# Two chained blocks in float32 on one core: row transposes and weight splits placed elsewhere around the attentions

## Time and profile before

| | |
|---|---|
| profiled execution, its own time | 2446.54 us |
| its span in the trace | 2444.8 us |
| median of the three runs | 2446.37 us |
| TensorE busy (matmuls) | 2380.5 us, 97% |
| VectorE busy | 1629.9 us, 67% |
| ScalarE busy | 1128.9 us, 46% |
| GpSimd busy | 167.0 us, 7% |
| share of TensorE in the chain that ended last | 88% |
| mean granted TensorE clock | 0.999 of full |

### The profile page before, as it was taken

One profiled execution on the slowest core, in us unless ns is written; L12 is line 12 of the kernel. 1 busy time (PEld: TensorE's weight loads), 2 busy tenths in 40 slices (PEclk: granted clock), 3 DMA queues, 4 the chain that ended last, 5 costly groups with the idle time before them and its releaser, 6 DMA issues.

```text
span 2444.8 us, 33463 instructions
## 1 busy us (share of the span) xinstructions
PE 2380.5 (97%) x13600; PEld 2002.2 (82%) x13600; DVE 1629.9 (67%) x2282; ACT 1128.9 (46%) x1571; POOL 167.0 (7%) x182
## 2 busy tenths in 40 slices
PE   7999999999999999999999999999999989999999
PEld 5788887787888778887888878888888878888887
DVE  6766755547667576677776676777676666677664
ACT  3644344444443434436434355564443454574442
POOL 2100002021000320000100100000100000001000
PEclk9999999999999999999999999999999999999999
DMA  6365343343553445543654344344754434444652
GB/s 233 134 215 206 138 172 138 138 173 134 194 206 138 173 166 196 207 158 123 244 203 161 128 172 170 140 174 146 275 206 156 151 115 162 173 173 168 235 172 89
DMA packets 258776, 419.08 MB, mean 171 GB/s; under 512 B 11937, under 2 KB 149153, under 8 KB 258625
## 3 DMA queue, kind: packets, MB, share of 16 engines
q1 hardware_dynamic: 253760, 400.15, 46.4%
q0 software_dynamic: 4864, 16.80, 1.9%
HBM read 415.86 MB, written 1.05 MB: 171 GB/s over the span
## 4 chain that ended last, share of the span: by engine, by line
PE 88%; DVE 6%; ACT 3%; issue 2%; DMA 1%; POOL 1%; SPq 0%; DVEq 0%; ACTq 0%
PE bank_L L2343 19%; PE bank_L L2359 17%; PE bank_S L2688 7%; PE bank_T L2653 7%; PE bank_L L2653 7%; PE bank_O L2688 7%; PE bank_T L2658 4%; PE bank_L L2658 4%; PE bank_L L2340 4%; DVE wlo L1565 2%; PE bank_O L2343 1%; PE bank_O L2605 1%; PE bank_S L2343 1%; ACT whi L1188 1%; PE bank_T L2300 1%
## 5 line engine op out<-in xcount | busy, mean ns | idle before, releaser
L1565 DVE TENSOR_TENSOR wlo<-raw,whi 128x2048 fp32r<-128x2048 f32 x316 | 713.7, 2279 | 149.2 <-ACT whi L1188 148.8
L1188 ACT ACTIVATE whi<-raw 128x2048 fp32r<-128x2048 f32 (+1 forms) x294 | 549.3, 1894 | 51.4 <-DMA raw<-in_w_in 12.9
L2343 PE MATMUL bank_L<-whi,xt 128*128 128x512 f32 (+1 forms) x1600 | 494.0, 391 | 4.5 <-DVE wlo L1565 2.5
L2359 PE MATMUL bank_L<-whi,xt 128*128 128x512 f32 x1280 | 400.2, 394 | 6.9 <-DVE wlo L1565 5.2
L2343 PEld LDWEIGHTS bank_L<-whi,xt 128*128 128x128 f32 x1600 | 293.5, 189 | 64.0 <-issue 4.5
L2343 PE MATMUL bank_L<-wlo,xt 128*128 128x512 f32 (+1 forms) x800 | 309.0, 386 | 0.0
L2359 PEld LDWEIGHTS bank_L<-whi,xt 128*128 128x128 f32 x1280 | 237.9, 189 | 56.7 <-issue 7.3
L2359 PE MATMUL bank_L<-wlo,xt 128*128 128x512 f32 x640 | 250.5, 391 | 0.0
L1440 ACT ACTIVATE tok<-tok 128x256 f32<-128x256 f32 x96 | 40.1, 417 | 450.6 <-DVE tok L2059 450.6
L2653 PE MATMUL bank_T<-xt,whi 128*128 128x512 f32 x768 | 192.3, 392 | 0.0
L2653 PE MATMUL bank_L<-xt,whi 128*128 128x512 f32 x768 | 191.7, 392 | 0.0
(11 more groups left out here) (344 smaller groups left out, 3654.4 us busy)
## 6 DMA issues: line engine op xcount, KB each, us to landing
raw<-in_w_gate_up SPq DMA_DIRECT2D x176, 512.0 KB, 5.7
raw<-in_w_in SPq DMA_DIRECT2D x72, 1024.0 KB, 7.0
draw<-in_w_down SPq DMA_DIRECT2D x44, 1024.0 KB, 5.8
raw<-in_ffn_w_up SPq DMA_DIRECT2D x88, 512.0 KB, 5.6
raw<-in_b_w_qkv SPq DMA_DIRECT2D x36, 1024.0 KB, 7.0
draw<-in_ffn_w_down SPq DMA_DIRECT2D x22, 1024.0 KB, 5.9
raw<-in_w_lift SPq DMA_DIRECT2D x16, 1024.0 KB, 6.2
raw<-in_a_w_qkv SPq DMA_DIRECT2D x12, 1024.0 KB, 8.8
```

The source lines that it names most:

```text
L1188: act.activation(wide(whi, w, nkc, ncols)[:, ks, :], wide(raw, w, nkc, ncols)[:, ks, :], ACT.Copy) \
L1565: dve.tensor_tensor(wide(wlo, w, nkc, ncols)[:, ks, :], wide(raw, w, nkc, ncols)[:, ks, :], wide(whi, w, nkc, ncols)[:, ks, :].bitcast(F32 ...
L2343: mm = pe.matmul(banks[name][:, 0:st["ncols"]], xx[:, kk, t * P:(t + 1) * P], ww[:, kk, :], start=(kk == 0 and q == 0), stop=(kk == nkc - ...
L2359: mm = pe.matmul(banks[bank][:, :], xx[:, k, t * P:(t + 1) * P], ww[:, k, :], start=(k == 0 and q == 0), stop=(k == KC - 1 and q == 2))
```

## The change

- **Second block, turns.** A new kind of stage, `turn_within`: the turns of `kd`, of the memory query and of the selected attention's query are issued by TensorE inside the product that stood ahead of them, at t = 1 and two k-steps from its end, and copied by ScalarE ahead of that product's second evacuation.
- **Memory attention.** `split_lo` of the lift chunk's halves goes from steps 1 and 4 to steps 4 and 5, the fourth `best` from step 5 to step 6. ScalarE's `split_hi` stays in steps 1 and 4.
- **Recurrence.** In the second layer VectorE makes the low part of the chunk of gate 0 half 1 inside `decay_logs`, ahead of its last four instructions instead of behind them.
- **Layers 0 and 3.** The rows leave by groups of four heads: TensorE turns group 0 after the values of unit 14, group 1 ahead of the values of unit 15, group 2 behind them, group 3 in the middle of the first output product. ScalarE copies groups 0 and 1 ahead of the output of unit 15. VectorE makes the low parts of groups 0, 1, 2, then the first half of chunk w+1, then group 3.
- GpSimd makes the high part of chunk w+1 (four casts per layer) in place of ScalarE.

```diff
@@ attention with sinks, where the stages are listed
-                o_is = attention(units, [(turn_done, n["turn"]), (dev, n["dev"])], first, behind, in_twos=True)
+                hv = halves(r)
+                pool_splits([n["w"] + 1])
+                attention(units, [(turn_done, n["turn"]), (dev, n["dev"])], first, behind, in_twos=True, turned=hv)
...
-            lhs = (tlo_done, [[hv["at"]["sg"] + k // 2 + 1 for k in range(KC)]] * T, (xt_hi, xt_lo)) if att else \
-                split(r, o_is, (xt_hi, xt_lo))
+            lhs = (tlo_done, [[hv["at"]["sg"] + k // 2 + 1 for k in range(KC)]] * T, (xt_hi, xt_lo))
...
-            lhs = renorm("layer", r, ALPHA, lhs, wo, bias, begun=att)
+            lhs = renorm("layer", r, ALPHA, lhs, wo, bias, begun=att, groups=hv)
@@ in attention(): when each group may be turned
+            if turned:
+                for g in range(4):
+                    turned["at_tp"][g] = n["tp"]
+                    turned["when"][g] = (o_done, n["unit"] + (g + 1) * len(units) // 4)
+                    n["tp"] += 1
@@ second block, where the stages are listed
-            turn(kd, kd_ok, kkT, 2)
+            turn_within(stages[-1], kd, kd_ok, kkT, 2)
...
-            turn(tc, q_ok, mqT, by=-128 ** -0.5)
+            turn_within(gate_st, tc, q_ok, mqT, by=-128 ** -0.5)
...
-            o_is = attention(units, [], (turn_done, n["turn"]), [], fill=[st], ps=ps2, rounds=(0, 2, 3, 5), left=2)
+            o_is = attention(units, [], (turn_done, n["turn"]), [], fill=[st], ps=ps2, rounds=(0, 2, 3, 6), left=2,
+                             lows={4: (n["w"], (0,)), 5: (n["w"], (1,))})
...
-            turn(tc, q_ok, dqT, by=BY)
+            turn_within(st, tc, q_ok, dqT, by=BY)
...
-            add("decay_logs", l=l, counts=counts, aev_z=n["aev"])
+            add("decay_logs", l=l, counts=counts, aev_z=n["aev"], w=n["w"] + 2)
@@ ScalarE, linear
+                        if st["within"]:
+                            heads_hi(st["within"])
                         evacuated(st, 1, LB[1])
@@ ScalarE, attention, step i
                             copies(i - 2)
+                        if st["rows"] and i == steps - 1:
+                            group_hi(st["rows"], 0)
+                            group_hi(st["rows"], 1)
                         if i >= 3:
                             evacuate(i - 3)
...
+                    if st["rows"]:
+                        group_hi(st["rows"], 2)
+                        group_hi(st["rows"], 3)
@@ ScalarE, select
+                    heads_hi(late["within"])
                     evacuated(late, 1, LB[1])
@@ VectorE, attention, end of step i, and after the last step
-                        if split_at(st["fill"], i, steps):
+                        if st["lows"] and i in st["lows"]:
+                            split_lo(*st["lows"][i])
+                        elif not st["lows"] and split_at(st["fill"], i, steps):
                             split_lo(*split_at(st["fill"], i, steps))
+                    if st["rows"]:
+                        for g in range(3):
+                            group_lo(st["rows"], g)
+                        split_lo(st["w"] + 1, (0,))
+                        group_lo(st["rows"], 3)
@@ VectorE, decay_logs
                     if k:
+                        split_upto(st["w"])
                         step.did(dve.tensor_tensor(headed(3), headed(3), by_channel[1], ALU.add))
@@ TensorE, product
+                    if st["within"] and t == 1 and k == nkc - 2:
+                        turn_heads(st["within"])
@@ TensorE, renorm
+                                elif t == 0 and h == 0 and st["groups"]:
+                                    three(*args, ALL[:KC // 2], first=True, rows=True)
+                                    turn_group(st["groups"], 3)
+                                    three(*args, ALL[KC // 2:], first=True, rows=True)
@@ TensorE, attention, step i
                             turned(i - 2)
+                        if st["rows"] and i == len(U) + 2:
+                            turn_group(st["rows"], 1)
                         if i >= 3:
                             values_(i - 3)
+                        if st["rows"] and i > len(U):
+                            turn_group(st["rows"], 2 * (i - len(U) - 1))
```

More of the change, by code:

```diff
@@ L256, in finishes, with renorm @@
                 fin[w] = n["lin"]
-        def renorm(norm, dst, alpha, lhs=None, weights=None, bias=False, begun=None):
+        def renorm(norm, dst, alpha, lhs=None, weights=None, bias=False, begun=None, groups=None):
             st = add("renorm", norm=norm, dst=dst, alpha=alpha, lhs=lhs, bias=bias, w=n["w"], gbv=n["gb"],
-                     rows=x if norm == "layer" else r, second=second[0] if lhs else None, begun=begun,
+                     rows=x if norm == "layer" else r, second=second[0] if lhs else None, begun=begun, groups=groups,
                      when=[(x_ready, n["xr"] + t + 1) for t in range(T)])
@@ L292, in linear @@
             st = add("linear", lhs=lhs, ncols=ncols, nkc=nkc, turned=turned, evac=evac, w=n["w"], mid=mid, inside=inside,
-                     func=func, narrow=narrow, after=after, into=into, inside_at=inside_at, skip=0, c0=0, whole=ncols, **kw)
+                     func=func, narrow=narrow, after=after, into=into, inside_at=inside_at, skip=0, c0=0, whole=ncols,
+                     within=None, **kw)
             chunks.append((loads, nkc, ncols))
@@ L306, in half_linear @@
             st = add("linear", lhs=lhs, ncols=NW, nkc=4, turned=False, evac="lift", w=w, mid=None, inside=None, into=into,
-                     c0=half * NW, whole=D, half=half, **kw)
+                     c0=half * NW, whole=D, half=half, within=None, **kw)
             for t in range(T):
@@ L344, in turn, with turn_within @@
             return st
+        def turn_within(late, src, ready, dst, nb_=4, by=1.0):
+            st = turn(src, ready, dst, nb_, by)
+            st["kind"], late["within"] = "turn_within", st
         def turn_inside(src, ready, dst, by=1.0):
@@ L370, in headnorm, with attention @@
             return (rope_done, n["rope"])
-        def attention(units, ready, first, behind, lead=2, in_twos=False, fill=(), ps=sm, rounds=(), shared=False, left=0):
+        def attention(units, ready, first, behind, lead=2, in_twos=False, fill=(), ps=sm, rounds=(), shared=False, left=0, lows=None, turned=None):
             add("attention", units=units, ready=ready, first=first, behind=behind, lead=lead, in_twos=in_twos,
-                fill=fill, ps=ps, qb=SB if fill else QB, rounds=rounds, left=left)
+                fill=fill, ps=ps, qb=SB if fill else QB, rounds=rounds, left=left, lows=lows, rows=turned, w=n["w"])
             for st in behind:
@@ L843, in build @@
             q_ok = rope(heads_of(tc, HD), 8, 1, dq_in)
-            linear(lhs, w_cols(C_AX), NW, "act", turned=True, dst=blk(0).rearrange("p (h s) -> p h s", s=SEQ), after=[])
-            turn(tc, q_ok, dqT, by=BY)
+            st = linear(lhs, w_cols(C_AX), NW, "act", turned=True, dst=blk(0).rearrange("p (h s) -> p h s", s=SEQ), after=[])
+            turn_within(st, tc, q_ok, dqT, by=BY)
             add("exp_table")
```

## The result

The changed kernel takes **2428.72 us** (median of 4 runs, 2428.42 to 2429.22); the kernel before took 2446.28 us beside it (4 runs). The ratio is 0.9929, 95% interval 0.9912 to 0.9946: 17.6 us less, where 16.4 was forecast. The profiled execution has a span of 2427.0 us against 2444.8, with a granted clock of 1.000 against 0.999.

What follows compares the result with a forecast made beforehand. TensorE, busy 97% of the span, was taken as the bound, so only its waits and slow stretches could be won: 12.2 + 2.4 + 0 + 0.5 + 1.3 = 16.4 us, giving 2430.0 us, range 2424.5 to 2437.

Steps and rivals of the forecast that it cites:

- The first rival's case: Whole kernel: the forecast as summed, 2430.0 us, its own range 2427 to 2433; chance 0.57.
- memory attention: Second block, both layers: waits of 0.79, 2.15 and 1.49 us and 1.67 of slow clock go, 6.10 per layer, 12.2 us.
- layers 0 and 3: End of attention: output product starts 1.97 us earlier, less costs of group 3; net 1.2 us per layer, 2.4 in all.
- query turn: Ahead of selected attention: visible wait 0.79 us, mostly hidden by ScalarE's table load; gains 0.27 per layer, 0.5 for both.
- decay: Recurrence, second layer: the 2.47 us wait goes, a new one of 1.1 to 1.2 ahead of C_GI comes; net 1.3 us.
- upper bound of 13.0: Memory attention, both layers: the gain if TensorE also saves the small steps between the waits, 13.0 instead of 12.2 us.
- The walk: Memory attention, step-by-step times: copies done before TensorE wants them, lift starts at 1471.45 (1477.2 before), 0.4 us to spare.
- My third rival: Clock still falls once per layer at a shorter gap: 2433.3 us, or 2436.3 with unit 3's wait kept; chance 0.20.
- My sign of "about 2 us": Layers 0 and 3: output product about 2 us after the last values instead of 3.8.
- GpSimd's casts: Layers 0 and 3: 0.85 us more on VectorE, covered by its 1.84 us idle; cost zero, bound 0.85 per layer.
- "What ScalarE sheds buys nothing": Layers 0 and 3: ScalarE's shed high part gains nothing, as TensorE has no wait in that output product.
- Key turn: Ahead of select: 0.80 us wait, but VectorE sets the fifth index score; gain 0, upper bound 1.6 for both layers.

## Why the prediction was right, and where its steps were off

Forecast 2430.0 (range 2424.5 to 2437.0), measured 2428.72. The first rival's case, the forecast itself, came. The mechanism held: the order of VectorE's work sets TensorE's waits. That the sum came within 1.3 us owes something to luck, as its terms missed by 1.2 (memory attention) and 0.5 (layers 0 and 3) and 0.5 (query turn) one way, and by 0.6 (the two losses) and 0.1 (decay) the other.

- **Memory attention**, forecast 6.10 per layer, measured 6.76 and 6.68. In the first layer the leads grow by 0.97 us up to the scores (0.79 forecast), 2.41 at unit 0's values (2.15), 1.65 for the half clock (1.67), 1.66 at unit 3's values (1.49) and 0.08 behind them: each step is a little more than its visible wait, and I had this only in the upper bound of 13.0 for both layers (13.4 measured). The walk had said this, 1477.2 against 1471.45, and I did not count it. Its copies come within 0.2 us of where it set them, once the lead of 3.72 at the scores is taken off. By the two runs that take the order alone, forward and backward, 10.6 to 11.0 of the 13.4 us are the order's; the turn ahead of the scores was not undone alone and has 0.97 and 0.92 in the ledger.
- **Why VectorE was late.** I wrote that VectorE is inside a low part before each late copy. That is half of it: before each low part it had stood idle, 2.97 and 2.58 us, for ScalarE's high half, which stands behind the exponentials of its step. In the second layer of the kernel before, ScalarE's row and then VectorE's:

```profile
1992.19 1.90 ACT L1188 ACTIVATE whi<-raw 128x2048 fp32r<-128x2048 f32 x1
...
1994.13 2.29 DVE L1565 TENSOR_TENSOR wlo<-raw,whi 128x2048 fp32r<-128x2048 f32 x1 [2.97 <-ACT whi L1188]
```

  In steps 4 and 5 of the changed kernel the high halves are ready when VectorE comes to them. Whether an earlier high half alone would have freed the copies in the old order was not tried.
- **Clock.** No fall in the trace of the changed kernel. My third rival rested on gaps of 1.0 to 1.5 us; the changed kernel has them (1.33, 1.34, 1.30) and the clock stays at 1.00 behind each, and so it does behind 1.48 in the run with both low parts in step 4. What I had wrong is that I took the fall as part of a 2.15 us gap: it comes behind some of these and not behind others, and it did not come behind the longer wait of 2.47 us in the recurrence, in any of the four traces that have it. The Trainium skill ("TensorE: Matmul & The Clock Gate", What's actually happening) says the window runs free of the kernel; the two layers of the run with the order undone agree with that. The same page's advice (HAM oscillation — how this bites in real kernels) names a longer gap than these as the one to avoid; here gaps of 1.95 and 2.15 us already brought the fall, and the measurement decides.
- **Layers 0 and 3**, forecast 1.2 each, measured 1.43 and 1.42. The product starts 2.2 us earlier, once the drift of 0.3 at the start is taken off, where I had 1.97. Group 2 stands behind group 0's low part with a wait of 0.57, and group 3 then costs its own time and 0.2 us for its late low part, as in the walk. My sign of "about 2 us" after the last values did not fit that walk, which gives 86.25 - 85.1 = 1.15; it is 0.95.
- **GpSimd's casts**, costed at zero with a bound of 0.85 per layer. In layer 0 zero held. In layer 3 the casts begin later, end at 1125.7 and reach VectorE's rope, where one instruction takes 0.73 us instead of 0.29; a turn then waits 0.21, and 0.3 us of the lead is gone. My cover was read in layer 0 alone.

```profile
1118.24 7.50 POOL L1141 CAST whi<-raw 128x1024 fp32r<-128x1024 f32 x4 [23.07 <-DMA raw<-in_a_w_o]
```

- **"What ScalarE sheds buys nothing"** was wrong as put. It buys no wait that the trace of before shows, but with the new order of VectorE the high part's time is on the path: made late it costs 10.6 us.
- **Key turn**, forecast 0: the lead gained at the first score, 0.8 us, is gone at the fifth. In the second layer 0.3 more goes there. The wait for VectorE's sums grew to 1.3 as forecast, at the third score and not at the fifth:

```profile
1433.86 0.71 PE L2790 MATMUL bank_S<-arena 64*128 64x128 f32 x8 [1.34 <-ACT arena L1517]
...
1438.08 1.13 PE L2790 MATMUL bank_S<-arena 64*128 64x256 f32 x8 [0.56 <-ACT arena L1517]
```

- **Query turn**, forecast 0.27 per layer, measured 0.52: half size. The failed step is the size of "moves up by 0.27". From the table load's start to the first exponential's it was 1524.91 - 1523.13 = 1.78 us; now it is 1514.89 - 1513.49 = 1.40, since the exponential waits for nothing behind the load's 1.28; that is 0.38, and the load itself starts 0.13 earlier than the lead of 9.51 gives.
```profile
1513.49 1.28 ACT L1264 ACT_TABLE_LOAD   x1
...
1514.89 0.39 ACT L1394 ACTIVATE sm<-sm,small 128x128 f32<-128x128 f32 x1
```

- **Decay**, forecast 1.3, measured 1.17 and undone 1.18. VectorE's L2223 starts 2.14 us after it was free, since ScalarE ends later, and the new wait is 1.30 where 1.1 to 1.2 was forecast:

```profile
2139.80 1.23 DVE L2223 TENSOR_TENSOR arena<-arena 128x1024 f32<-128x1024 f32 x1 [2.14 <-ACT arena L1541]
...
2145.66 4.49 DVE L1587 TENSOR_TENSOR wlo<-raw,whi 128x2048 fp32r<-128x2048 f32 x2
```

Left open: what decides, execution by execution, whether the clock falls behind a gap of about 2 us was not tried by itself. The drift in untouched parts arises at three places. At the start TensorE's rows run at half pace until 23 to 26 us, earlier in one execution and later in another. In layer 2 a turn waits 0.17 us for VectorE in the trace of after and 1.01 in the trace of before. And at layer 2's end TensorE waits 1.3 to 2.0 us behind VectorE, which itself waits for the transfer of a bias (`in_a_b_o`): 2.32 us in the trace of before, 2.48 in that of after, 3.00 in the run with the decay split back. Why these differ between executions is not shown.

## What to carry to other kernels

Where one engine serves both a fill (long splits) and a pipeline of copies, the long pieces belong between two copies, one at a time: the same two low parts make no wait in steps 4 and 5, cost 1.7 us per layer in one step, and in steps 1 and 4 they cost 4.1 us at full clock and 5.7 with the half clock. Look also at what such a piece itself waits for: an engine that works in order stands still at it, as VectorE did for 2.97 us. When a wait disappears, look at once for the wait that grew: taking up the index scores' 4.3 us gave another 3.9, and it took only splitting by halves. And before an engine's work is called free since nobody waits for it, ask what stands behind it once the order changes.

## What was not expected of the hardware

- Four GpSimd casts beside two VectorE subtractions of 128 x 2048 stretch the pair from 4.49 us to 5.33 and 5.90, and a small VectorE instruction of 0.29 to 0.73. The Trainium skill ("GPSIMD Engine Reference", Key points) names the contention; these are its sizes here.
- The granted clock fell at idle gaps of 1.95, 2.14 and 2.15 us (five times in the fourteen traces), at a cost of about 1.6 us each. It did not fall at gaps of 2.13 and 2.14 us in the other layer of two of the same executions, nor at the 2.47 us gap of the recurrence in any of four traces. At gaps up to 1.7 us it never fell, and at 4.0 us it did in both layers. So in these traces the length of a gap of about 2 us does not tell whether a fall comes. All this is past the first 50 us: at the start the rows show a clock of 1.00, although eight turns take 1.94 us there instead of 1.03, so in that stretch the column isn't to be trusted.
